# Two Fourier tiles with tokens on the partitions, positions before channels, and other homes and turns for expert pieces in a float32 transformer kernel

## The reference, cut to what matters

```python
def fourier_mix(u):
    bsz, s, _ = u.shape                                   # s = 256, 512 channels
    f = u.astype(jnp.float32).reshape(bsz, s, FOURIER_GROUPS, FOURIER_GROUP_DIM)   # 4 groups of 128
    y = jnp.fft.fft2(f, axes=(1, 3), norm='ortho').real
    return y.reshape(bsz, s, D_FOURIER)

h = rmsnorm_2(x, norm1_g)
p = jnp.einsum('bsd,dn->bsn', h, w_in)                    # 1024 -> 3 x 512
lru_x, lru_gate, four_in = p[..., :512], p[..., 512:1024], p[..., 1024:]
c = centred_depthwise_conv(lru_x, conv_w, conv_b)
h_f, h_b = rglru(c, ..., reverse=False), rglru(c, ..., reverse=True)
y_lru = jax.nn.gelu(lru_gate) * (h_f + h_b)
mixed = jnp.concatenate([y_lru, fourier_mix(four_in)], axis=-1)
x = x + mixed @ w_out                                     # 1024 -> 1024
h2 = rmsnorm_2(x, norm2_g)
x = x + expert_choice_moe(h2, w_router, w_gate, w_up, w_down)   # 16 experts, 24 MB of weights each
return rmsnorm_2(x, normf_g)
```

## Time and profile before

| | |
|---|---|
| median of 3 runs | 2106.16 us (2105.23 to 2107.66) |
| the profiled execution | 2106.13 us, of which the profile's span is 2104.3 us |
| TensorE busy | 1827.6 us (87%) |
| VectorE busy | 810.1 us (38%) |
| ScalarE busy | 599.7 us (28%) |
| GpSimd busy | 131.4 us (6%) |
| moved | 603.69 MB, mean 287 GB/s |

### The profile page before, as it was taken

One profiled execution on the slowest core, in us unless ns is written; L12 is line 12 of the kernel. 1 busy time (PEld: TensorE's weight loads), 2 busy tenths in 40 slices (PEclk: granted clock), 3 DMA queues, 4 the chain that ended last, 5 costly groups with the idle time before them and its releaser, 6 DMA issues.

```text
span 2104.3 us, 30777 instructions
## 1 busy us (share of the span) xinstructions
PE 1827.6 (87%) x13304; PEld 1349.9 (64%) x13304; DVE 810.1 (38%) x950; ACT 599.7 (28%) x706; POOL 131.4 (6%) x139
## 2 busy tenths in 40 slices
PE   8999999999999999999999996676677677577676
PEld 8999997999999997599999732122222112122221
DVE  7655557765665564767658500000000000000000
ACT  6333546533433354654327300000000000000001
POOL 4200011400000000220001000000000000000000
PEclk9999999999999999999999997788887888879878
DMA  8555452555555454166556999999999999999997
GB/s 272 180 179 170 154 187 97 177 183 191 186 194 192 154 184 128 39 196 215 179 186 233 414 428 428 428 428 428 429 429 429 429 428 428 429 428 429 429 429 331
DMA packets 182536, 603.69 MB, mean 287 GB/s; under 512 B 11952, under 2 KB 139440, under 8 KB 158016
## 3 DMA queue, kind: packets, MB, share of 16 engines
q1 hardware_dynamic: 180560, 601.43, 73.6%
q10 hardware_dynamic: 1648, 0.70, 0.1%
q0 software_dynamic: 256, 0.52, 0.1%
HBM read 601.58 MB, written 1.05 MB: 286 GB/s over the span
## 4 chain that ended last, share of the span: by engine, by line
PE 61%; DMA 35%; DVE 2%; ACT 1%; issue 0%; SPq 0%; ACTq 0%; POOL 0%; DVEq 0%; POOLq 0%
PE ps L1075 22%; DMA bulk<-in_w_up 15%; PE ps L1089 12%; DMA bulk<-in_w_down 8%; DMA bulk<-in_w_gate 8%; PE ps L1252 3%; PE ps L1656 3%; PE ps L1684 2%; DMA keep<-in_w_up 2%; DMA keep<-in_w_down 2%; PE ps L1146 2%; PE ps L1041 2%; PE ps L1145 2%; PE ps L1147 2%; PE ps L1155 1%; PE ps L1157 1%
## 5 line engine op out<-in xcount | busy, mean ns | idle before, releaser
L1075 PE MATMUL ps<-part,part 128*128 128x256 f32 x3840 | 460.1, 280 | 1.4 <-DVE part L2250 1.4
L1075 PEld LDWEIGHTS ps<-part,part 128*128 128x128 f32 x3840 | 455.5, 188 | 1.8 <-DVE part L2250 1.6
L1656 PE MATMUL ps<-bulk 128*32 128x512 f32 x1616 | 254.8, 763 | 146.2 <-DMA bulk<-in_w_up 89.5
L2250 DVE TENSOR_TENSOR part<-bulk,part 128x2048 fp32r<-128x2048 f32 x88 | 203.5, 2354 | 221.3 <-ACT part L1750 221.3
L1656 PEld LDWEIGHTS ps<-bulk 128*32 128x32 f32 x1616 | 50.8, 125 | 331.0 <-issue 134.0
L1089 PE MATMUL ps<-part,part 128*128 128x256 f32 x2112 | 255.5, 280 | 0.0
L1089 PEld LDWEIGHTS ps<-part,part 128*128 128x128 f32 x2112 | 251.8, 188 | 0.0
L1750 ACT ACTIVATE part<-bulk 128x2048 fp32r<-128x2048 f32 x86 | 160.1, 1910 | 227.0 <-DMA bulk<-in_ffn_w_up 227.0
L2884 DVE TENSOR_TENSOR keep<-keep,ps 128x512 f32<-128x512 f32 x16 | 11.0, 688 | 527.6 <-PE ps L1656 527.6
L1684 PE MATMUL ps<-bulk,keep 128*32 128x512 f32 x784 | 113.7, 714 | 31.0 <-DMA bulk<-in_w_down 30.6
L2259 DVE TENSOR_TENSOR part<-bulk,part 128x2048 fp32r<-128x2048 f32 x45 | 103.4, 2312 | 46.6 <-ACT part L1765 46.6
(11 more groups left out here) (328 smaller groups left out, 2218.1 us busy)
## 6 DMA issues: line engine op xcount, KB each, us to landing
bulk<-in_w_gate SPq DMA_DIRECT2D x53, 2048.0 KB, 40.6
bulk<-in_w_up SPq DMA_DIRECT2D x48, 2048.0 KB, 40.3
bulk<-in_w_down SPq DMA_DIRECT2D x48, 2048.0 KB, 40.3
bulk<-in_ffn_w_gate SPq DMA_DIRECT2D x44, 1024.0 KB, 5.5
bulk<-in_ffn_w_up SPq DMA_DIRECT2D x44, 1024.0 KB, 8.0
bulk<-in_ffn_w_down SPq DMA_DIRECT2D x44, 1024.0 KB, 5.4
keep<-in_w_up SPq DMA_DIRECT2D x16, 2048.0 KB, 40.7
keep<-in_w_down SPq DMA_DIRECT2D x15, 2048.0 KB, 40.5
```

The costliest lines, as they stand in the source:

```text
L1075: ins = pe.matmul(y, w_, x_, start=(k == m == 0), stop=(k == KD - 1 and m == 2))
L1656: ins = pe.matmul(ps[j * CAP:(j + 1) * CAP, half, :], xe[:, k, :], w[:, kk, j * HALF:(j + 1) * HALF], start=(k == 0), stop=(k == KD - 1))
L2250: dve.tensor_tensor(hi(slot(3 * b + i)), slot(3 * b + i), as32(w_hi(f, b, i)), ALU.subtract).then_inc(gu_split, 1)
```

## The change

1. The Fourier part is projected with tokens on the partitions: the stationary operand is 128 tokens of the normed input, the moving one 256 columns of the weight. Two PSUM tiles `fo0`, `fo1` (one for each 128 tokens, 512 channels) take the place of four; the weight piece 5 comes first, then 4. The factor of each token is now a column: `four_columns` makes it out of `rrow` and the identity, `four_taken` multiplies it in.
2. The transform over positions comes first (`fa0`, `fa1`: 8 plain products of 256 columns, cosines and sines of half the positions side by side), then that over channels (`fb0`, `fb1`: 4 products of 258 or 254 columns). `fold`, the small one-row products and the memset of `fodd` fall away; `four_sums` makes the two mirrored halves out of the even and the odd part instead. ScalarE rounds them (`four_high`) two tiles at a time, and VectorE makes the low parts (`four_lows`), now from on-chip memory.
3. TensorE's order after the gates: `fa0`, `fa1`, `lg2`, `lg3`, `fb0`, `fb1`, `lg0`, `lg1`, `project_out`. VectorE's and ScalarE's orders follow.
4. Homes: the gelu tiles, `four`, `four_s`, `normf` and `xe` move, the scans write over their input, one `w_out` piece has another slot, and the arena is 104 words larger. Pieces 2 to 6 of the experts have other buffers, and SP's program other waits and another order of issues.

```diff
-NFOUR = 256 + 2 * T
+NFOUR = 2 * P + TT * T
...
-            w = (1, 2, "x", 7, 8, 4, "mem", 0, 3, 6, 5)[b]
+            w = (1, 2, 7, 8, "x", "mem", 4, 0, 3, 6, 5)[b]
...
-        for i in range(CT):
-            plan(f"fo{i}", g % 8, "dve")
-            g += 1
+        for t in range(TT):
+            plan(f"fo{t}", 4 + t, "dve")
+        g = 0
...
-                    plan(f"l{w}{dr}{i}", g % 8, "act")
+                    plan(f"l{w}{dr}{i}", (0, 1, 2, 3, 6, 7, 4, 5)[g % 8], "act")
...
+                    if key == ("wout2", WOUT2[2]):
+                        mix_slot_free(sp, slot_no[("win2", 3)])
+                    elif n >= MIX_SLOTS and key != ("wout2", WOUT2[3]):
                         mix_slot_free(sp, n - MIX_SLOTS)
...
             sp.wait_ge(dn_used, NFFN * NCH - 1)
-            mix_loads(NMLA + 8, NMLA + 9)
 
             for i in range(12):
                 if i == 1:
                     mix_loads(NMLA + 5, NMLA + 7)
-                    sp.wait_ge(tile_done, done("fo3"))
+                    sp.wait_ge(four_half, 1)
                 if i == 2:
                     sp.wait_ge(dn_used, NFFN * NCH)
                     sp.wait_ge(tile_done, done("li13"))
                     sp.dma_start(normf, A["normf_g_2"].partition_broadcast(P)).then_inc(normf_loaded, 16)
+                    sp.wait_ge(l_ic, 2)
+                if i == 3:
+                    sp.wait_ge(tile_done, done("fa1"))
+                    mix_loads(NMLA + 8, NMLA + 9)
                     mix_loads(NMLA + 7, NMLA + 8)
-                    sp.wait_ge(tile_done, done("lg3"))
-                if i == 3:
-                    sp.wait_ge(tile_done, done("fa3"))
-                    sp.wait_ge(l_ic, 2)
+                    sp.wait_ge(tile_done, done("fb1"))
                 if i == 4:
-                    sp.wait_ge(tile_done, done("fb3"))
-                if i == 6:
-                    sp.wait_ge(lru_out, 2)
-                if i in (5, 7, 8, 9):
-                    sp.wait_ge(wout_used, CAT + (1, None, 2, 3, 4)[i - 5])
+                    sp.wait_ge(tile_done, done("lg1"))
+                if i == 5:
+                    sp.wait_ge(l_mul, 2)
+                if 6 <= i < 10:
+                    sp.wait_ge(wout_used, CAT + i - 5)
...
-                    pe.wait_ge(*((four_low, 2 * n + 2) if n < 2 else (lru_out, n - 1)))
+                    pe.wait_ge(*((four_low, n + 1) if n < 2 else (lru_out, n - 1)))
...
-            for i in range(CT):
-                gate_or_four("fo", i)
+            def four_rows(c):
+                w_h, w_l = weights(("win2", 4 + c))
+                for t in range(TT):
+                    if c:
+                        begin(f"fo{t}")
+                    y = tbank(f"fo{t}")[:, c * CW:(c + 1) * CW]
+                    for k in range(KD):
+                        x_h, x_l = [part[:, k, t * P:(t + 1) * P] for part in XNT]
+                        pe.matmul(y, x_h, w_h[:, k, :], start=(c == 1 and k == 0), stop=False, skip_group_check=True)
+                        pe.matmul(y, x_h, w_l[:, k, :], start=False, stop=False, skip_group_check=True)
+                        ins = pe.matmul(y, x_l, w_h[:, k, :], start=False, stop=(k == KD - 1), skip_group_check=True)
+                    if c == 0:
+                        end(ins)
+                return ins
...
+            def over_positions(b):
+                begin(f"fa{b}")
+                for i in range(2):
+                    for t in range(TT):
+                        ins = pe.matmul(tbank(f"fa{b}")[:, i * T:(i + 1) * T], four[:, t, (2 * b + i) * P:(2 * b + i + 1) * P],
+                                        fc[:, 2 * P + t * T:2 * P + (t + 1) * T], start=(i == t == 0), stop=(t == 1),
+                                        skip_group_check=True)
+                end(ins)
...
+            def over_channels(b):
+                begin(f"fb{b}")
+                pe.wait_ge(*out_of(f"fa{b}"))
+                even_, odd_ = halves(f"fb{b}")
+                pair = four_s[:, 2 * b:2 * b + 2, :]
+                pe.matmul(even_, fc[:, 0:P], pair[:, :, 0:P + 1], start=True, stop=True, skip_group_check=True)
+                end(pe.matmul(odd_, fc[:, P:2 * P], pair[:, :, P + 1:T], start=False, stop=True, skip_group_check=True))
+
+            four_rows(1).then_inc(four_half, 1)
+            four_rows(0)
...
-            for i in range(CT):
-                gate_or_four("lg", i)
             pe.wait_ge(four_loaded, 16)
...
-            pe.wait_ge(*out_of("lg3"))
+            for t in range(TT):
+                pe.wait_ge(*out_of(f"fo{t}"))
+            over_positions(0)
+            over_positions(1)
+            gelu_branch((2, 3))
+            over_channels(0)
+            over_channels(1)
+            gelu_branch((0, 1))
+            pe.wait_ge(*out_of("fb1"))
             project_out()
...
-            lru_root(0)
-            lru_root(1)
+            for b in range(2):
+                lru_root(b)
+                act.wait_ge(*out_of(f"fb{b}"))
+                pair = slice(CT + 2 * b, CT + 2 * b + 2)
+                act.activation(hi(mixH)[:, pair, :], mixT[:, pair, :], ACT.Copy).then_inc(four_high, 1)
             act.activation(small[:, 46:47], epsc, ACT.Gelu_apprx_tanh)
-            for i in range(CT):
-                evac(f"fb{i}", hi(mixH)[:, CT + i, :])
+            for i in (2, 3, 0, 1):
                 act.wait_ge(*out_of(f"lg{i}"))
                 act.activation(gel[:, i, :], gel[:, i, :], ACT.Gelu_apprx_tanh).then_inc(gel_done, 1)
...
+            def four_columns():
+
+                for t in range(TT):
+                    dve.scalar_tensor_tensor(out=four[:, t, 0:P], in0=rrow[:, t * P:(t + 1) * P], scalar=1.0, in1=ident, op0=ALU.mult,
+                                             op1=ALU.mult, accum_out=fcol[:, t:t + 1]).then_inc(four_col, 1)
+
+            def four_taken(t):
+
+                dve.wait_ge(four_col, t + 1)
+                dve.wait_ge(tile_done, done(f"fo{t}"))
+                dve.tensor_scalar(four[:, t, :], tbank(f"fo{t}"), fcol[:, t:t + 1], None, ALU.mult).then_inc(dve_out, 1)
+
+            def four_sums(b):
+
+                y, of = mixT[:, CT + 2 * b:CT + 2 * b + 2, :], tbank(f"fb{b}")
+                even_, odd_ = [of[:, i:j].rearrange("p (i s) -> p i s", i=2) for i, j in ((0, 2 * P + 2), (2 * P + 2, 4 * P))]
+                dve.wait_ge(tile_done, done(f"fb{b}"))
+                first, mirrored = y[:, :, 1:P], y[:, :, P + 1:T][:, :, ::-1]
+                dve.tensor_copy(mirrored, odd_).then_inc(four_odd, 1)
+                dve.tensor_copy(y[:, :, 0:P + 1:P], even_[:, :, 0:P + 1:P])
+                dve.wait_ge(four_odd, 2 * b + 1)
+                dve.tensor_tensor(first, even_[:, :, 1:P], mirrored, ALU.subtract).then_inc(four_odd, 1)
+                dve.wait_ge(four_odd, 2 * b + 2)
+                dve.tensor_tensor(mirrored, even_[:, :, 1:P], mirrored, ALU.add).then_inc(dve_out, 1)
...
-                dve.wait_ge(gel_done, 2 * h + 2)
+                dve.wait_ge(gel_done, CT)
...
-            for i in range(CT):
-                scaled(f"fo{i}", four[:, i, :])
+            four_columns()
+            four_taken(0)
+            four_taken(1)
             split_mix(("win2", 3))
+            input_gated(0)
             split_mix(("wout2", WOUT2[0]))
-            fold()
+            input_gated(1)
+            for b in range(2):
+                evac(f"fa{b}", flat(four_s[:, 2 * b:2 * b + 2, :]), tbank(f"fa{b}"))
             split_mix(("wout2", WOUT2[1]))
-            input_gated(0)
-            input_gated(1)
             one_minus_square(0)
+            scaled("lg2", gel[:, 2, :])
+            scaled("lg3", gel[:, 3, :])
+            four_sums(0)
+            one_minus_square(1)
+            four_sums(1)
+            four_lows(0)
             scaled("lg0", gel[:, 0, :])
-            scaled("lg1", gel[:, 1, :])
-            scaled("lg2", gel[:, 2, :])
-            one_minus_square(1)
-            scaled("lg3", gel[:, 3, :])
-            for i in range(CT):
-                evac(f"fa{i}", fab[:, i, :])
             scaled_input(0)
             scaled_input(1)
+            four_lows(1)
+            scaled("lg1", gel[:, 1, :])
             dve.wait_ge(l_mul, 2)
-            four_lows(0, 2)
             scans(0, 0)
             scans(1, 0)
             gated_half(0)
-            four_lows(2, 4)
             scans(0, 1)
```

More of the change, by code:

```diff
@@ L150, in place @@
             return ctx.enter_context(nc.sbuf_tensor(name, [P, n], F32)), at
-        ARENA = 18328
+        ARENA = 18432
         bulk, bulk_at = place("bulk", 10 * SLOT + ARENA)
-        keep, keep_at = place("keep", 52736 - 10 * SLOT - ARENA)
+        keep, keep_at = place("keep", 52840 - 10 * SLOT - ARENA)
         wring = bulk[:, 0:10 * SLOT]
@@ L699, in program @@
         conv = v3(9248, CT, T)
-        gel = memT[:, CT:KD, :]
-        four = v3(11296, CT, T)
-        fab = v3(12320, CT, 2 * P)
-        fodd = v3(15648, CT, P)
+        gel = v3(16384, CT, T)
```

(25 more changed lines are left out.)

80 lines of the change are left out of this document (31 added, 49 removed).

## The result

Over 22 runs each on the same chips the kernel before takes 2105.95 us (2104.41 to 2107.66) and the changed one 2109.06 us (2107.61 to 2111.46): ratio 1.0015, 95% interval 1.0009 to 1.0021. That is 3.1 us slower, inside the bound of 0.2% and against a forecast of 2.8 us faster (2103.3 us). The profiled execution took 2110.97 us with a span of 2108.9 us, 1.9 us above its own median, so a local step read from it is counted from a landmark near it, not from the start of the span. Two places in the trace can hold most of the 1.9 us: TensorE's granted clock is at its lower level (1.2 instead of 2.4 GHz) for a stretch near 12 us (0.59 and 0.56 in the slices 10 to 12 and 12 to 14 us) and for another near 257 us (0.53 from 256 to 258 us). The profiled execution of the kernel before has only the second one (0.50 there).

A forecast was written before the change was run, and what follows sets the result against it. Expert weight transfers bound the kernel; their unbroken stream restarts at the later of queue end (1198.6) and first-use data (1200.2), 2.8 us before 1203.0. So 2106.13 - 2.8 = 2103.3 us, range 2100.9 to 2107.0.

The forecast's parts named there:

- any shift before 1127 us, which nothing in the change explains: Sign listed as showing the forecast wrong: work ahead of the changed part moving in time; no size or chance given.
- The transform: TensorE between gates and `project_out`: 7.26 us removed, 5.4 us added as 12 plain products, gain taken as 1.9 us.
- The projection at zero: Fourier projection keeps 96 products of 256 columns; tokens stationary and weight piece 5 first cost zero.
- VectorE's chain: VectorE's work up to the last split before `project_out`'s fourth piece: ends about 1178.5, wanted 1180.1, cover 1.6 us.
- SP's queue: SP's issues of `w_out` and expert pieces 2 to 10: done at 1198.6, 4.4 us earlier than 1203.0.
- The sum of the restart: Expert stream restarts at the later of queue (1198.6) and piece 11's data after first use (1200.2), 2.8 us earlier.
- only TensorE's part: Rival: the first use binds already before the change, so only TensorE's 1.9 us is gained, 2104.2 us; chance 0.20.
- the queue's 0.9: Before the change the expert queue ends 0.9 us after first-use data could flow; an earlier queue alone gains at most that.
- A wait eats the gain: Rival: new handovers on TensorE's path add 1.9 us of waiting, leaving 0.9 us from the queue, 2105.2 us; chance 0.14.
- the ceiling: Rival: TensorE gains 3.6 us or more, the queue at 1198.6 limits, gain 4.4 us, 2101.7 us; chance 0.09.
- the late chain: Rival: VectorE's chain 7 us longer delays `project_out`'s fourth piece, 2.6 us slower, 2108.7 us; chance 0.09.
- The stream's rate: Expert weight transfers: trace rate of 427 to 428 GB/s assumed unchanged, against the skill's 358 GB/s.

The follow-up runs named there:

- b_both: Kernel before with only the two homes moved as the change moves them (small buffer up 104 words, `xT_lo` down 16): 2111.22 us.
- a_128: Changed kernel with 32 unused words ahead of each of the large and small buffers, offsets (128, 0): 2095.48 us.
- b_128: Kernel before with 32 unused words ahead of the large buffer, 136 ahead of the small, `xT_lo` at 6144, offsets (128, 0): 2097.95 us.

## Why the prediction was wrong

The forecast was 2.8 us faster and the kernel is 3.1 us slower. Point by point:

- **The step that failed** is one of the change's list that the sum does not have: the homes. "Other homes" were followed for who waits for whom, and the arena's 104 words and the 16 words of `xT_lo` were given no price at all. The sum so put the effect of the moved operands on the unedited products before 1127 us at nothing, without a reason. They cost 5.3 us by themselves (`b_both`) and turn -2.8 into about +2.5; 3.1 was measured. The prediction did name the sign of it, "any shift before 1127 us, which nothing in the change explains", but took it for impossible and gave it no chance. Something in the change did explain it.
- **The transform** was right: from `R6`, `project_out` starts 1.8 us earlier (1.9 forecast), and it takes 23.04 us where 23.2 was said.
- **The projection at zero** was right within 0.2 us: from `R6` to the gates it is 1139.20 - 1127.5 = 11.7 us before and 1146.08 - 1134.2 = 11.9 after.
- **VectorE's chain** held. In its timeline the mirrored halves cost no more than forward ones, 0.42 us for 254 elements, and the last split still ended ahead of its need: 1182.57 + 2.28 = 1184.85 for a piece whose first product starts at 1186.70, a cover of 1.8 us where 1.6 was said. VectorE's timeline of the kernel after, one `four_sums` and the last split:

```profile
1163.01 0.42 DVE L2752 COPY bulk<-ps 128x254 f32<-128x254 f32 x1 [0.44 <-PE ps L1540]
1163.35 0.16 DVE L2753 COPY bulk<-ps 128x4 f32<-128x4 f32 x1
1163.46 0.42 DVE L2755 TENSOR_TENSOR bulk<-ps,bulk 128x254 f32<-128x254 f32 x1
1163.92 0.42 DVE L2757 TENSOR_TENSOR bulk<-ps,bulk 128x254 f32<-128x254 f32 x1
...
1182.57 2.28 DVE L2297 TENSOR_TENSOR part<-bulk,part 128x2048 fp32r<-128x2048 f32 x1
```

- **SP's queue** was right in order, and about 1 us too early in the sum: the pause before piece 11 was to be 1.6 us and is worth 0.6. Small pauses lie between the earlier pieces: 344 GB/s from 1158 to 1160 us, 350 and 358 from 1162 to 1166 us. Since the first use binds, this cost nothing.
- **The sum of the restart**, the later of queue and first use, is right in place and size: 2.7 us in the profile, 2.5 us in the timed pair `a_128` and `b_128`. Of the rivals, "only TensorE's part" (1.9) is nearest, but the earlier issue of 2.0 us and the 2.7 us of the stream say that some of the queue's 0.9 came too; the timed pair (2.5 us) is between the two and does not decide. "A wait eats the gain", "the ceiling" and the late chain did not come about: no new wait stands on TensorE in this stretch.
- **The stream's rate** is 428 GB/s again. The Trainium skill, "DMA: Bandwidth & Descriptors", section "Bandwidth", says that the memory side, about 358 GB/s for a core, binds such transfers; this trace does not agree, and after the change as before the measured rate decides. The same section gives 425 GB/s for 16 MB moved by one core whose neighbour is idle, and this kernel, on one core, fits that figure. (At 358 GB/s the prediction's queue would end nearer 1208 than 1206 us, by the same estimate; nothing hangs on it.)

What stays open: by what mechanism the two slow pairs of offsets cost their 1 to 1.6 ns for each gate and up product, why neither offset does it alone, why the same pair acts otherwise on the projection products, by what the start of the large buffers sets the stream's rate, and what is left of the 3.1 us. The two measured parts, 5.3 to 5.6 and -2.5, sum to 2.8 to 3.1, and the rest lies within the intervals of the ratios (0.1% is 2.1 us).

## What to carry to other kernels

An edit that moves a buffer is an edit of every instruction that reads it. Ask of each new size and each new start which unedited loops read what lies behind it, and hold the page's busy time of those loops against the old one before anything in the changed stretch is explained. The median weight load is not enough: it showed one slow pair (192 ns for 188) and missed the slower one (188). To judge a change that moves homes, measure it on equal homes, and try a few starts of the large buffers by themselves: here they were worth up to 12.7 us, the change 2.5.

## What the runs showed of the hardware

- A dense row of products 128x128 by 128x256, each with its own weight load, has a pace that depends on the pair of offsets (modulo 256 bytes) of its moving operands against the stationary ones. In the gate and up products it is 118.8 ns at (0, 0) and 119.4 at (64, 0), and 117.4 to 117.9 at the six other pairs that ran. In the projection products the order is another: 1288 of them take 154.0 us at (0, 0), 150.8 at (64, 0) and 148.1 at (64, 64).
- With the large buffer, which holds seven of the ring's nine, at a multiple of 256 bytes the stream runs at 431 GB/s instead of 428 (611.2 instead of 614.9 ns for a packet of 16 KB), 6 us over its 890 us, even where the other two begin 64 or 128 bytes past such a multiple. A multiple of 512 adds nothing.
- The granted clock can be at its lower level for a short stretch in one execution and not in another of the same kind: from 256 to 258 us it is 0.50 in the kernel before and 1.00 in `b_both`, and TensorE was busy for 3.49 of the 4 us before 254 in both. It moves `R6` by 0.6 to 1.4 us.
- Results that VectorE writes in reversed order take no longer: 254 elements in 0.42 us. A forward copy of 256 elements out of PSUM takes 0.42 us in the same kernel (at 850.99 us).
